# The borders between stages of a two-block network kernel on one core, and its expert scatter

## The chip, the cores and the metric

The kernel runs on one core of a Trainium2 chip. A core has TensorE (PE in the rows; PEld is its load of weights), VectorE (DVE), ScalarE (ACT), GpSimd (POOL) and SyncE (SP, which here only issues DMAs). The metric is the device time in microseconds (us) of one execution, as the median of several.

## The reference, cut to what matters

256 tokens of 1024 features, all fp32, pass through two blocks. The parts follow each other, and each border between two of them is a residual sum and a norm:

```python
def rmsnorm(x, g):
    xf = x.astype(jnp.float32)
    xf = xf * lax.rsqrt(jnp.mean(xf * xf, axis=-1, keepdims=True) + EPS)
    return (xf * g.astype(jnp.float32)).astype(x.dtype)

# block 1 (16 meta tokens in front; they are dropped at its end)
h = h + hybrid_mixer(rmsnorm(h, g_mix), ...)        # ends in  y @ w_out      (2048 -> 1024)
h = h + peer_ffn(rmsnorm(h, g_ffn), ...)            # ends in  act @ expert_v (16384 -> 1024)
h = rmsnorm(h, g_final)
# block 2
h = h + hgrn2_mixer(rms_norm(h, hg_norm), ...)      # ends in  o @ w_out
h = h + conv_ffn(rms_norm(h, ffn_norm[0]), ...)     # ends in  (silu(conv) * val) @ w_down
h = h + swa_sink_attention(rms_norm(h, attn_norm), shared_kv(h, kv_norm), ...)   # ends in  out @ w_o
h = h + conv_ffn(rms_norm(h, ffn_norm[1]), ...)
return rms_norm(h, final_norm)

# peer_ffn, its middle: 8 heads pick 16 of 16384 experts each, expert = i1 * 128 + i2
act = gelu(einsum('td,tkd->tk', xb, u)) * gates
out = einsum('tk,tkd->td', act, expert_v[experts])
```

So there are six such borders after the first norm: w_out to PEER, PEER to HGRN2 (two norms in a row: g_final, then hg_norm), HGRN2 to FFN 0, FFN 0 to attention, attention to FFN 1, and FFN 1 to the output.

## The kernel before, in words

**Slabs.** All weights come as a stream of 524 slabs of 128 x 1024 fp32. SP loads them into a ring of four. Each is split in two: ACT writes the rounded upper part (`split_hi`, L234) and DVE the remainder (`split_lo`, L242), three slabs ahead of their use. A product of two such splits takes three matmuls. An `up` slab (L258 to L260) makes 128 output features for all 256 tokens: 8 steps over k, 24 matmuls into one of two banks, which ACT or DVE must empty before its turn comes again. A `down` slab (L319 to L321) takes 128 input features and adds to all 1024 outputs of both token tiles: 12 matmuls into the four banks 4 to 7, which hold the sum over the whole stage. Its input y is split as well (yhi by ACT, ylo by DVE: L467 and L472; L1907 and L1944 in the FFNs), two slabs ahead.

**A border.** When the first token tile of the last down slab is done, DVE adds banks 4 and 5 to h, and after the slab banks 6 and 7 (`add_dve`, L451); it then splits one more slab. ACT squares and sums each tile of h (L372); DVE makes mean plus eps, ACT the root, DVE the reciprocal (L381, L376, L384), each for both tiles in one instruction; DVE scales tile 0 and ACT tile 1 (L391, L396). Then PE transposes 8 x 2 squares of 128 x 128 (`norm_pe`, L411) into banks 4 to 7, ACT multiplies by the gain into xhi (L430), DVE makes xlo (L437), and the first up slab may start, step k when part k of xlo is there. From PEER to HGRN2 the kernel does the sums, the mean and the root twice, with a product in between that writes the new h (L1701). There the old h is also fetched back from HBM: three DMAs on POOL's queue, the last of which waits for the last ylo.

**Clearing.** `clear_accumulators` (L302) runs four matmuls of one row of zeros over banks 4 to 7 ahead of each down stage, and PE waits until they are done. In the FFNs, where up and down slabs alternate, it stands between the first two up slabs.

**PEER.** 128 up slabs give the activations of all 16384 experts, which are stored to HBM; 128 down slabs use them. Beside up slabs 64 to 127 the gates are scattered: G, for token t and columns i1, i2, is a product of two one-hot matrices made from lists of 128 picks. In each of 64 steps there are one up slab and four tokens. DVE makes the left one-hot with the gate on it (L1378, one instruction a token, two buffers); POOL copies four columns (L1456) and makes the right one-hot (L1462, one instruction a token, four buffers); PE multiplies them (L1177), two tokens in the middle of the up slab and two behind it. ACT copies the result of four tokens, 128 x 512, to G (L1241), which is laid out token by token, so that later the factor of down slab k is read with a stride of 128 elements (L1398).

The order of work on each engine is the order of the code; semaphores tie the engines together. Loops are unrolled by four.

## Time and profile before

| | us |
|---|---|
| median of 3 runs | 1847.3 (1847.25 to 1850.32) |
| the profiled execution | 1850.21 |
| its span, first to last instruction | 1848.3 |
| PE busy in it | 1739.4 (94%) |
| DVE busy | 1266.9 (69%) |
| ACT busy | 962.1 (52%) |
| POOL busy | 415.7 (22%) |

In the rows, times are us from the span's start. PE's instructions overlap, so that the distance between two starts counts, not the length. "Idle before" is the idle time of that engine ahead of the instruction, with what ended it. PEclk is the granted TensorE clock as a share of 2.4 GHz.

### The profile page before, as it was taken

To read this page: it belongs to the slowest core of one execution; us is meant where nothing else is said; L and a number is where in the kernel's file an instruction comes from. 1 tells how busy PE (TensorE), PEld (TensorE's weight loads), DVE (VectorE), ACT (ScalarE), POOL (GpSimd) and SP (SyncE) were. 2 spreads that over 40 slices of the span, in tenths; PEclk is the share of its full clock that TensorE was granted. 3 is DMA by queue.
4 is the path that set the end of the run, shared out by engine and by line. 5 is a ranking of instruction groups with operands and counts; after the bars stand their busy time and mean duration, and the time that the engine had idled before them with its cause. 6 is when DMAs were issued, how large, how long until landed. Compare 5 with 4: busy or idle time off the path is not lost.

```text
span 1848.3 us, 36609 instructions
## 1 busy us (share of the span) xinstructions
PE 1739.4 (94%) x11651; PEld 1590.8 (86%) x11651; DVE 1266.9 (69%) x2118; ACT 962.1 (52%) x1455; POOL 415.7 (22%) x430
## 2 busy tenths in 40 slices
PE   7999999998989999999999998999899998789998
PEld 6998879998989999988888886988699998679997
DVE  5866664588976666678888887698566665556565
ACT  6653345666644444445555554654455555555554
POOL 0022300234268888810000000066000000100000
PEclk9999999999999999999999999999899999999999
DMA  5542255577764444567777777433255554135553
GB/s 182 169 137 81 74 188 182 166 211 212 214 193 163 156 157 158 166 209 240 242 242 241 241 241 247 142 119 110 100 161 183 184 189 132 35 119 187 185 181 112
DMA packets 114423, 316.59 MB, mean 171 GB/s; under 512 B 12768, under 2 KB 45920, under 8 KB 113984
## 3 DMA queue, kind: packets, MB, share of 16 engines
q1 hardware_dynamic: 113360, 311.88, 53.0%
q0 software_dynamic: 1008, 4.00, 0.7%
q8 instruction: 32, 0.52, 0.1%
q14 instruction: 23, 0.19, 0.0%
HBM read 296.95 MB, written 18.87 MB: 171 GB/s over the span
## 4 chain that ended last, share of the span: by engine, by line
PE 81%; DVE 10%; ACT 3%; issue 3%; POOL 2%; DMA 1%; POOLq 0%; DVEq 0%; ACTq 0%; SPq 0%
PE bank L258 13%; PE bank L260 13%; PE bank L259 13%; PE bank L319 10%; PE bank L320 10%; PE bank L321 10%; PE bank L1177 3%; DVE wlo L242 2%; POOL ylo L1462 1%; PE bank L1591 1%; PE bank L411 1%; DVE arena L1754 1%; PE bank L883 1%; ACT arena L372 1%; ACT whi L234 1%
## 5 line engine op out<-in xcount | busy, mean ns | idle before, releaser
L242 DVE TENSOR_TENSOR wlo<-raw,whi 128x1024 fp32r<-128x1024 f32 x502 | 640.1, 1277 | 199.2 <-ACT whi L234 189.5
L258 PE MATMUL bank<-xhi,whi 128*128 128x256 f32 (+1 forms) x2424 | 707.2, 292 | 15.9 <-DVE wlo L242 9.2
L260 PE MATMUL bank<-xhi,wlo 128*128 128x256 f32 (+1 forms) x2424 | 691.4, 285 | 0.0
L259 PE MATMUL bank<-xlo,whi 128*128 128x256 f32 (+1 forms) x2424 | 691.0, 285 | 0.0
L234 ACT ACTIVATE whi<-raw 128x1024 fp32r<-128x1024 f32 x524 | 550.9, 1052 | 116.1 <-PE bank L321 65.6
L258 PEld LDWEIGHTS bank<-xhi,whi 128*128 128x128 f32 x2424 | 468.1, 193 | 26.3 <-issue 13.7
L259 PEld LDWEIGHTS bank<-xlo,whi 128*128 128x128 f32 x2424 | 468.2, 193 | 1.7
L260 PEld LDWEIGHTS bank<-xhi,wlo 128*128 128x128 f32 x2424 | 467.3, 193 | 0.0
L319 PE MATMUL bank<-whi,yhi 128*128 128x512 f32 x816 | 322.2, 395 | 2.3 <-DVE ylo L1406 1.3
L320 PE MATMUL bank<-wlo,yhi 128*128 128x512 f32 x816 | 320.9, 393 | 0.0
L321 PE MATMUL bank<-whi,ylo 128*128 128x512 f32 x816 | 320.2, 392 | 0.0
L1462 POOL TENSOR_SCALAR ylo<-iota,tiny 128x128 fp32r<-128x128 f32 x256 | 214.1, 852 | 20.2 <-PE bank L1177 14.4
L319 PEld LDWEIGHTS bank<-whi,yhi 128*128 128x128 f32 x816 | 155.2, 190 | 36.6 <-DVE ylo L472 2.6
L321 PEld LDWEIGHTS bank<-whi,ylo 128*128 128x128 f32 x816 | 155.0, 190 | 32.8
L320 PEld LDWEIGHTS bank<-wlo,yhi 128*128 128x128 f32 x816 | 155.2, 190 | 30.3
L1214 ACT ACTIVATE h<-bank 128x256 f32<-128x256 f32 x128 | 49.1, 384 | 206.2 <-PE bank L260 206.0
L1259 ACT ACTIVATE yhi<-h 128x256 fp32r<-128x256 f32 x128 | 53.4, 418 | 173.2 <-PE bank L321 169.5
L1378 DVE TENSOR_SCALAR h<-iota,h 128x128 f32<-128x128 f32 x256 | 85.8, 368 | 73.6 <-PE bank L1177 73.0
L1406 DVE TENSOR_TENSOR ylo<-h,yhi 128x256 fp32r<-128x256 f32 x128 | 54.4, 425 | 68.0 <-ACT yhi L1259 68.0
L1177 PE MATMUL bank<-ylo,h 128*128 128x128 f32 x512 | 84.3, 282 | 11.4 <-POOL ylo L1462 11.4
L1927 DVE SCALAR_TENSOR_TENSOR arena<-bank,vec,arena 128x255 f32<-128x255 f32 x88 | 42.4, 482 | 71.8 <-ACT arena L1892 65.8
L1437 POOL TENSOR_TENSOR wlo<-raw,whi 128x1024 fp32r<-128x1024 f32 x22 | 53.5, 2432 | 145.3 <-ACT whi L234 121.6
(255 smaller groups left out, 1563.5 us busy)
## 6 DMA issues: line engine op xcount, KB each, us to landing
raw<-in_stream SPq DMA_DIRECT2D x524, 512.0 KB, 3.5
act_spill<-h SPq DMA_DIRECT2D x128, 128.0 KB, 3.2
h<-act_spill SPq DMA_DIRECT2D x128, 128.0 KB, 3.4
h<-in_x SPq DMA_DIRECT2D x1, 1024.0 KB, 5.1
arena<-in_keys POOLq DMA_DIRECT2D x1, 1024.0 KB, 5.9
h_spill<-h SPq DMA_DIRECT2D x1, 1024.0 KB, 8.5
out<-arena SPq DMA_DIRECT2D x2, 512.0 KB, 2.7
h<-h_spill POOLq DMA_DIRECT2D x2, 256.0 KB, 5.1
```

The costliest lines, as they stand in the source:

```text
L234: nc.scalar.activation(whi[:, q * 1024:(q + 1) * 1024], raw[:, q * 1024:(q + 1) * 1024], ACT.Copy).then_inc(hi_ready, 1)
L242: nc.vector.tensor_tensor(wlo[:, q * 1024:(q + 1) * 1024], raw[:, q * 1024:(q + 1) * 1024], whi[:, q * 1024:(q + 1) * 1024].bitcast(F32), ...
L258: nc.tensor.matmul(bank[b][:, 0:T], whi[:, w], xhi[:, x], start=k == 0, stop=False)
L259: nc.tensor.matmul(bank[b][:, 0:T], whi[:, w], xlo[:, x], start=False, stop=False)
L260: last = nc.tensor.matmul(bank[b][:, 0:T], wlo[:, w], xhi[:, x], start=False, stop=k == KT - 1)
L319: nc.tensor.matmul(o, yhi[:, y], whi[:, w], start=False, stop=False, skip_group_check=True)
L320: nc.tensor.matmul(o, yhi[:, y], wlo[:, w], start=False, stop=False, skip_group_check=True)
L321: last = nc.tensor.matmul(o, ylo[:, y], whi[:, w], start=False, stop=True, skip_group_check=True)
L1177: nc.tensor.matmul(o, HOT1[:, y % 2 * P:(y % 2 + 1) * P], HOT2[:, y * P:(y + 1) * P].bitcast(F32), start=True, stop=True).then_inc(s("hot_ ...
L1378: nc.vector.tensor_scalar(HOT1[:, y % 2 * P:(y % 2 + 1) * P], iota[:, :], c1(I1T), c1(GT_COLS), ALU.is_equal, ALU.mult).then_inc(s("hot_a" ...
L1406: nc.vector.tensor_tensor(ylo[:, yq * SEQ:(yq + 1) * SEQ], PRD[:, yq * SEQ:(yq + 1) * SEQ], yhi[:, yq * SEQ:(yq + 1) * SEQ].bitcast(F32), ...
L1462: nc.gpsimd.tensor_scalar(HOT2[:, y * P:(y + 1) * P], iota[:, :], PCOL[:, y:y + 1], None, ALU.is_equal).then_inc(s("hot_b"), 1)
```

## The change: borders tile by tile, and the scatter's right one-hot on VectorE

It does six things.

1. The last two down slabs of a stage are taken together: both for token tile 0, then both for tile 1 (`down_last`). A semaphore tells of each of banks 4, 5 and 6, and the last slab's own of bank 7.
2. The norm of a border goes by tile, and for tile 1 by half (`turn_dve`, `turn_act`, `turn_pe`): tile 0 has its own root, reciprocal, scaling and transposes. Eps goes into ACT's bias. The transposes go to banks 2 to 6. The split of slab last + 3 stands after the norm on both engines, not in the middle of it and ahead of it.
3. From PEER to HGRN2 the two norms are one: DVE multiplies the sum by g_final (u), ACT squares and sums both h and u, and the root is of a combination of the two sums. The new residual is made later, beside the second and third HGRN2 slabs. The old h and g_final are fetched when 52 of the 128 products of the down stage are made, into a part of G that is used up by then.
4. The output is multiplied by its gain before the root is known, and leaves in three DMAs.
5. No clearing matmuls: the first down matmul into each bank starts it anew.
6. The right one-hots of four tokens are made by one DVE instruction, a comparison of iota and the columns, both broadcast, into two buffers of four tokens (ylo and yhi) in turn. POOL does none of it. ACT writes G transposed, expert by expert, and the factor of down slab k is contiguous.

```diff
+        def down_last(pe, n, d):
+            for tt in range(TT):
+                for z in range(2):
+                    q, yq = slot(n + z, 0), (d + z) % 2
+                    if tt == 0:
+                        pe.wait_ge(lo_ready, n + z + 1)
+                        pe.wait_ge(y_lo, d + z + 1)
+                    y = slice(yq * SEQ + tt * P, yq * SEQ + (tt + 1) * P)
+                    for nh in range(2):
+                        last = down_half(bank[4 + 2 * tt + nh][:, :], y, nh, q, False)
+                        if z and 2 * tt + nh < 3:
+                            last.then_inc(bank_done, 1)
+                    if tt:
+                        last.then_inc(slabs_done, 1)
...
+            add(0)
+            add(1)
+            gain(0, D, 1)
+            add(2)
+            gain(D, D + 512, 2)
+            if a == T_HG:
+                dve.wait_ge(turn_ss, ss_base(a) + 2)
+                nc.vector.scalar_tensor_tensor(out=TV[:, 0:1], in0=TSS[:, 0:1], scalar=EPS, in1=TSS[:, 1:2],
+                                               op0=ALU.mult, op1=ALU.add).then_inc(turn_v, 1)
+            add(3)
+            gain(D + 512, 2 * D, 3)
+            dve.wait_ge(turn_rt, 2 * a + 1)
+            nc.vector.reciprocal(TRS[:, 0:1], TRT[:, 0:1]).then_inc(turn_rs, 1)
+            dve.wait_ge(turn_rs, 2 * a + 1)
+            nc.vector.tensor_scalar(nt[:, 0:D], turn_src(a)[:, 0:D], TRS[:, 0:1], None, ALU.mult)\
+                .then_inc(turn_nt, 1)
+            dve.wait_ge(turn_ss, ss_base(a + 1))
...
+            act.wait_ge(h_done, 4 * a + 2)
+            square(0, D, 0)
+            square_u(0, D, 0, 1)
...
+            act.wait_ge(h_done, 4 * a + 3)
+            square(D, D + 512, 2)
+            square_u(D, D + 512, 2, 2)
+            act.wait_ge(h_done, 4 * a + 4)
+            square(D + 512, 2 * D, 4)
+            square_u(D + 512, 2 * D, 4, 3)
...
+            pe.wait_ge(h_done, 4 * a + 4)
+            pe.wait_ge(turn_nt, 2 * a + 1)
+            for j in range(KT):
+                nc.tensor.transpose(turned(j)[:, 0:P], nt[:, j * P:(j + 1) * P], ident[:, :])
+            pe.wait_ge(turn_nt, 2 * a + 2)
+            for j in range(KT):
+                if j == KT // 2:
+                    pe.wait_ge(turn_nb, a + 1)
+                last = nc.tensor.transpose(turned(j)[:, P:SEQ], nt[:, D + j * P:D + (j + 1) * P], ident[:, :])
...
-                dst = G[:, k * w:(k + 1) * w] if isinstance(k, int) else G[:, bass.ds(k * w, w)]
-                nc.scalar.activation(dst, bank[2 + r % 2][:, 0:w], ACT.Copy).then_inc(s("g_evac"), 1)
+                n = (i * 4 + r) * TPS
+                g3 = G[:, :].rearrange("p (k t) -> p t k", t=SEQ)
+                dst = g3[:, n:n + TPS, :] if isinstance(n, int) else g3[:, bass.ds(n, TPS), :]
+                nc.scalar.activation(dst, bank[2 + r % 2][:, 0:TPS * KEYS].rearrange("p (t k) -> p t k", k=KEYS),
+                                     ACT.Copy).then_inc(s("g_evac"), 1)
...
+            def four_tokens(k0, i, r):
+                n = i * (4 * TPS) + (k0 + r) * TPS
+                c4 = I2T[:, n:n + TPS] if isinstance(n, int) else I2T[:, bass.ds(n, TPS)]
+                nc.vector.tensor_tensor(HOT2[(k0 + r) % 2][:, :].rearrange("p (t k) -> p t k", k=P),
+                                        iota[:, :].unsqueeze(1).to_broadcast([P, TPS, P]),
+                                        c4.unsqueeze(2).to_broadcast([P, TPS, P]),
+                                        ALU.is_equal).then_inc(s("hot_b"), 1)
...
-            for part, free, count in ((slice(6 * SEQ, 8 * SEQ), s("hot_free"), SEQ + TPS), (slice(0, 4 * SEQ), y_new, KEYS),
-                                      (slice(4 * SEQ, 6 * SEQ), y_lo, D_V + KEYS)):
-                pool.wait_ge(free, count)
-                pool.dma_start(h[:, part], t["h_spill"][:, part]).then_inc(s("h_back"), 16)
+            pool.wait_ge(y_new, 13 * D // SEQ)
+            pool.dma_start(H_OLD, t["h_spill"]).then_inc(s("h_back"), 16)
+            pool.dma_start(G_FINAL, t["g_final"]).then_inc(s("row_in"), 16)
```

PE at the first border, w_out to PEER, in program order. Before (L321 is the last matmul of the last down slab, L411 the transposes, L258 the first up matmul):

```order
L321 MATMUL bank<-whi,ylo 128x512
L112 REGISTER_ALU
L112 COMPARE_AND_BRANCH
L411 MATMUL bank<-ident,arena 128x128 [waits nt_done]
L411 MATMUL bank<-ident,arena 128x128 x15
L258 MATMUL bank<-xhi,whi 128x256 [waits nlo_done,up_evac,lo_ready]
```

And now (L303 the last down matmul, L542 the transposes of tile 0, L547 those of tile 1, L259 the first up matmul):

```order
L303 MATMUL bank<-whi,ylo 128x512
L542 MATMUL bank<-ident,arena 128x128 [waits turn_nt,h_done]
L542 MATMUL bank<-ident,arena 128x128 x7
L547 MATMUL bank<-ident,arena 128x128 [waits turn_nt]
L547 MATMUL bank<-ident,arena 128x128 x3
L547 MATMUL bank<-ident,arena 128x128 [waits turn_nb]
L547 MATMUL bank<-ident,arena 128x128 x3
L259 MATMUL bank<-xhi,whi 128x256 [waits nlo_done,up_evac,lo_ready]
```

One wait for both tiles became three, and the transposes of tile 0 stand ahead of the wait for tile 1.

DVE at the same border. Before (L451 the sums, L242 a slab's split, L381 and L384 the mean and the reciprocal, L391 the scaling of tile 0, L437 xlo):

```order
L242 TENSOR_TENSOR wlo<-raw,whi 128x1024 [waits hi_ready]
L451 TENSOR_TENSOR h<-h,bank 128x512 [waits halves_done]
L451 TENSOR_TENSOR h<-h,bank 128x512
L451 TENSOR_TENSOR h<-h,bank 128x512 [waits slabs_done]
L451 TENSOR_TENSOR h<-h,bank 128x512
L242 TENSOR_TENSOR wlo<-raw,whi 128x1024 [waits hi_ready]
L381 TENSOR_SCALAR tiny<-tiny 128x2 [waits ss_done]
L384 RECIPROCAL tiny<-tiny 128x2 [waits rt_done]
L391 TENSOR_SCALAR arena<-h,tiny 128x1024 [waits rs_done]
L437 SCALAR_TENSOR_TENSOR xlo<-bank,vec,xhi 128x256 [waits nhi_done] x8
```

And now (L452 the sums, L472 to L474 root, reciprocal and scaling of tile 0, L483 to L487 those of tile 1, L570 xlo, L243 the split):

```order
L243 TENSOR_TENSOR wlo<-raw,whi 128x1024 [waits hi_ready]
L452 TENSOR_TENSOR h<-h,bank 128x512 [waits bank_done] x3
L452 TENSOR_TENSOR h<-h,bank 128x512 [waits slabs_done]
L472 RECIPROCAL tiny<-tiny 128x1 [waits turn_rt]
L474 TENSOR_SCALAR arena<-h,tiny 128x1024 [waits turn_rs]
L483 TENSOR_TENSOR tiny<-tiny 128x1 [waits turn_ss]
L485 RECIPROCAL tiny<-tiny 128x1 [waits turn_rt]
L487 TENSOR_SCALAR arena<-h,tiny 128x512 [waits turn_rs]
L570 SCALAR_TENSOR_TENSOR xlo<-bank,vec,xhi 128x256 [waits nhi_done] x8
L243 TENSOR_TENSOR wlo<-raw,whi 128x1024 [waits hi_ready]
```

The split of slab last + 3 moved from behind the sums to behind xlo.

DVE in a step of the scatter, now (L1488 the left one-hot of a token, L1494 the right ones of the next step's four; before, the rows were the same without L1494):

```order
L1488 ISA [waits hot_free]
L1488 TENSOR_SCALAR h<-iota,h 128x128
L242 ISA
L243 TENSOR_TENSOR wlo<-raw,whi 128x1024 [waits hi_ready]
L1486 REGISTER_ALU
L1488 ISA [waits hot_free]
L1488 TENSOR_SCALAR h<-iota,h 128x128
L1486 REGISTER_ALU
L1488 ISA [waits hot_free]
L1488 TENSOR_SCALAR h<-iota,h 128x128
L1494 ISA
L1494 TENSOR_TENSOR yhi<-iota,h 128x512
```

The added comparison stands behind the second pair of tokens and ahead of the next step's first.

## Rows read from the trace of the kernel before

**Rows 1.** The page, the chain that ended last, by engine:

```profile
PE 81%; DVE 10%; ACT 3%; issue 3%; POOL 2%; DMA 1%; POOLq 0%; DVEq 0%; ACTq 0%; SPq 0%
```

**Rows 2.** Waits of the whole program: who for whom, total us, times, longest:

```profile
PE bank L411 <- ACT arena L396: 29.2, 5, 11.7
PE bank L1177 <- POOL ylo L1462: 11.4, 15, 2.0
```

**Rows 3.** PE in one turn of the scatter's loop: start, length, instruction, idle before:

```profile
614.87 0.38 PE L258 MATMUL bank<-xhi,whi 128*128 128x256 f32 x1
...
617.75 0.36 PE L258 MATMUL bank<-xhi,whi 128*128 128x256 f32 x1
...
619.64 0.36 PE L258 MATMUL bank<-xhi,whi 128*128 128x256 f32 x1
...
631.42 0.38 PE L258 MATMUL bank<-xhi,whi 128*128 128x256 f32 x1
```

**Rows 4.** Groups of instructions from 540 to 780 us (busy, mean ns, idle before):

```profile
L1378 DVE TENSOR_SCALAR h<-iota,h 128x128 f32<-128x128 f32 x236 | 79.2, 368 | 66.6 <-PE bank L1177 66.4
L242 DVE TENSOR_TENSOR wlo<-raw,whi 128x1024 fp32r<-128x1024 f32 x59 | 74.3, 1260 | 24.2 <-ACT whi L234 24.2
L234 ACT ACTIVATE whi<-raw 128x1024 fp32r<-128x1024 f32 x59 | 62.2, 1054 | 1.6
L1241 ACT ACTIVATE arena<-bank 128x512 f32 x59 | 34.6, 587 | 0.0
L1214 ACT ACTIVATE h<-bank 128x256 f32<-128x256 f32 x59 | 22.6, 383 | 130.4 <-PE bank L260 130.4
```

**Rows 5.** Single lines of the program: ns min/median/max, first and last start:

```profile
L1298 DVE TENSOR_TENSOR arena<-arena x16: 417/422/1870, 384.9 to 493.5; 128x256 f32<-128x256 f32 x16
L1318 DVE TENSOR_TENSOR arena<-iota,arena x4: 2284/2285/2286, 414.3 to 507.6; 128x2048 f32<-128x2048 f32 x4
L1398 DVE TENSOR_TENSOR h<-h,arena x128: 595/629/642, 796.4 to 1140.7; 128x256 f32<-128x256 f32 x128
```

**Rows 6.** The border from HGRN2 to FFN 0, in order of time:

```profile
1333.22 0.39 PE L321 MATMUL bank<-whi,ylo 128*128 128x512 f32 x1
...
1336.78 1.15 ACT L396 ACTIVATE arena<-h,tiny 128x1024 f32<-128x1024 f32 x1 [0.23 <-DVE tiny L384]
1336.78 0.75 DVE L391 TENSOR_SCALAR arena<-h,tiny 128x1024 f32<-128x1024 f32 x1
1337.98 3.68 PE L411 MATMUL bank<-ident,arena 128*128 128x128 f32 x16 [4.38 <-ACT arena L396]
...
1340.01 3.44 DVE L437 SCALAR_TENSOR_TENSOR xlo<-bank,vec,xhi 128x256 fp32r<-128x256 f32 x8 [2.47 <-ACT xhi L430]
...
1341.31 0.56 PE L258 MATMUL bank<-xhi,whi 128*128 128x256 f32 x1
...
1345.55 1.04 PE L302 MATMUL bank<-tiny 1*128 1x512 bf16 x4
...
1346.65 0.39 PE L258 MATMUL bank<-xhi,whi 128*128 128x256 f32 x1
```

**Rows 7.** The border from PEER to HGRN2:

```profile
1147.63 0.39 PE L321 MATMUL bank<-whi,ylo 128*128 128x512 f32 x1
...
1163.00 0.42 PE L258 MATMUL bank<-xhi,whi 128*128 128x256 f32 x1
...
1167.96 0.38 ACT L1636 ACTIVATE arena<-bank 128x256 f32<-128x256 f32 x1
```

**Rows 8.** The end of FFN 0, and the end of the program:

```profile
1528.45 0.47 PE L319 MATMUL bank<-whi,yhi 128*128 128x512 f32 x1 [0.15 <-DVE ylo L1944]
...
1842.70 2.48 DVE L2154 SCALAR_TENSOR_TENSOR arena<-h,tiny,arena 128x1024 f32<-128x1024 f32 x2
```

**Rows 9.** Stretches: PE, PEld, DVE, ACT, POOL busy (count), PEclk, DMA share, GB/s:

```profile
1340.00:1344.00 4.00, 4.00 (x20) 4.00 (x19) 3.92 (x9) 3.45 (x7) 0.00 (x0) 0.50 0.07 27
940.00:960.00 20.00, 20.00 (x90) 16.57 (x89) 16.21 (x23) 9.65 (x15) 0.00 (x0) 1.00 0.75 243
```

461 lines of the change are left out of this document (241 added, 220 removed).

## The prediction

> **What bounds the kernel now.** I read the page first: the chain that ended last is PE for 81%, DVE for 10% [rows 1]. So PE's work is the bound, and what can be won is where PE stands idle or works at half clock. The waits say where [rows 2]: PE's transposes (L411) waited 29.2 us for the norm's last scaling at five borders, 11.7 of them at one, so 4.4 us at each of the four others; and the scatter's matmuls (L1177) waited 15 times for POOL. Then I read these places in order of time [rows 3, 6, 7], and for each resource that the change uses more the groups, single lines and stretches [rows 4, 5, 9]. In the down stage of PEER, and in the long up loops, PE does not wait (20.00 us busy of 20.00 in rows 9), so faster DVE work there is worth nothing.
>
> **The scatter.** A half step (12 up matmuls and two tokens) takes PE 619.64 - 617.75 = 1.89 us without a wait, and 617.75 - 614.87 = 2.88 with the wait for POOL [rows 3]. There is one such wait in each turn of four steps, which takes 631.42 - 614.87 = 16.55 us. 14 waits of this kind (the 15th is the first step's, 2.0 us, rows 2) at 1.0 are 14.0 us. What is late next, once POOL is out? DVE gets one comparison of 512 elements a step. The nearest row is L1318, the same comparison of two broadcasts on 2048 elements, 2285 ns, so 571 ns for 512 [rows 5]. A step's DVE work becomes 4 x 0.37 + 1.26 + 0.57 = 3.3 us [rows 4] against PE's 3.78. The comparison stands where DVE now waits for PE before the next token (66.4 us over 236 tokens, 1.1 us a step, rows 4), needs no buffer that PE has not long left, and so costs nothing up to about 1 us. ACT writes G with a stride of 1 KB: the price is in no row. Its bounds: 0.59 us as now [rows 4], and above, as the strided read L1398 is to the contiguous L1298 (629 to 422 ns, rows 5), 0.88 us; three times as much, 1.8 us, would still fit, since ACT has 1.05 + 0.59 us and a copy of 0.4 in a step of 3.78. I take 0.6 to 0.9, no cost. The first step's wait of 2.0 us shrinks to what DVE needs for its comparison, about 0.4: 1.6 won. Sum 15.6 us. Ends: 8 (DVE or ACT sometimes late by half a us) and 18 (halves just behind the stall, a tenth late, become normal as well).
>
> The Trainium skill speaks against the strided write: in "SBUF — State Buffer", section "Door 1: The DMA port swizzle", each access that crosses to a new 16-byte line pays a penalty, and an fp32 stride of over four elements does so every time. The read with a stride of 128 elements shows such a penalty on DVE, a half more [rows 5]; no row shows a write by ACT. By the rule the read gets cheaper and the write dearer; both stay beside PE's work, so the sum would be the same by the one as by the other.
>
> **One plain border, worked out on HGRN2 to FFN 0** [rows 6]. T is the end of the last down matmul, 1333.61. Before: scaling at T+3.2, the transposes at T+4.4 and the first up matmul at T+7.7; an up slab at full clock takes 2.85 us (24 x 0.119, half a step less its tokens), so it ends at T+10.5. After, with a sum of 512 columns 0.65 us, a square of 1024 columns 1.2 and of 512 0.75, a root, a reciprocal and each handover 0.2: banks 4 and 5 are done at T-3.4 and T-2.7; DVE is still at a split and has both sums at T-1.4; ACT's square and root end at T+0.2; DVE has bank 6's sum at T and bank 7's at T+0.7; reciprocal, then 0.75 for scaling tile 0 [rows 6]: T+1.65. PE starts its transposes at T+1.7 instead of T+4.4. ACT meanwhile squares the two halves of tile 1 until T+1.5; sum, root, reciprocal, and the half scalings on DVE and ACT together end at T+2.9, while PE is at tile 0 (8 x 0.2). PE ends the transposes at T+4.9. xlo then sets the pace, 3.44/8 = 0.43 a part against PE's 0.36: its first part is there at T+4.6, its last at T+7.9, and the first up slab ends at T+8.2. Won: 2.3 us. Ends: 1.2, if half clock falls on the up slab, and 3.
>
> The clock: in this border it was at 0.50 over 4 us after PE had been idle for 4.38 [rows 6, 9], and the first up slab took 1345.46 - 1341.31 = 4.15 us. After the shorter idle time of 1.7 us it may fall or not; I count on full clock in the up slab here (1.3 more won) and let the range hold the other case.
>
> What the moved split gives back: on ACT behind xhi now stand two splits, so that in the FFNs the convolution's first product comes at T+9.1, not at once, and DVE, with two splits behind xlo, ends its two taps at T+11.6. They empty the bank for the third up slab, which PE could start at T+11.0: 0.6 lost at both FFN borders. In PEER and attention ACT's copy comes at T+9.5, in time.
>
> The six borders: w_out to PEER 2.3. HGRN2 to FFN 0: 2.3 + 1.3 - 0.6 = 3.0. Attention to FFN 1: 2.3 - 0.6 = 1.7. FFN 0 to attention: here the last down slab began at 1528.45, when its ylo came, about 3.1 us after the slab before it had begun [rows 8], for DVE makes a split before this ylo. Now that ylo is wanted 1.36 us (half a down slab) after that beginning, so PE waits there, and 18 matmuls, not 12, stand behind it: 6 x 0.227 = 1.4 lost, 0.9 left. FFN 1 to output has no split there: 0.25 lost.
>
> PEER to HGRN2 [rows 7]: T is 1148.02. Before: first up matmul at T+15.0, and the third slab, which needs the Sigmoid of the first (ends at 1168.34, T+20.3), right behind the second, at T+20.8. After: h is there early, so no DMA ends any wait. The products with g_final (0.65 for 512 columns, 1.2 for 1024) and the squares of u double both engines' lists: tile 0 is scaled at T+3.2, tile 1 at T+5.8, the first up matmul at T+7.4. But ACT then has a split, two roots, the load of two function tables and another split ahead of the Sigmoid, DVE a split ahead of the small lower-bound work that ACT's Exp waits for: xhi ends at T+9.5, Sigmoid at T+15.4. So the third slab begins at T+15.5: 5.3 won, not the 7.6 that the first up matmul shows. Ends: 4 and 7.
>
> Output: before, the last scaling ended at 1842.70 + 2.48 = T+5.7 [rows 8] and the span 3.1 later. After, the chain goes add, gain, square, sum, root, reciprocal, half scaling: T+4.35, but SP issues three DMAs one behind the other (about 0.7 each), the last at T+5.0: 0.7 won, less the 0.25 above: 0.5.
>
> **No clearing.** From the clearing's start to the next up matmul 1346.65 - 1345.55 = 1.1 us [rows 6]; it is on PE's path in both FFNs and ahead of w_out: 3.3. Ahead of the HGRN2 and attention down stages PE waits for ylo beside it, 0.4 each. Ahead of PEER's down stage ylo comes 1.3 later anyway: 0. Sum 4.1.
>
> **Fetching h and g_final early** puts 1.5 MB into a stage that uses 0.75 of the DMA engines' time [rows 9]. The spare quarter of 243/0.75 = 324 GB/s takes it in about 19 us, and the loads run four slabs ahead. Cost 0; if it is not spread so, at most 1.5 MB / 243 GB/s = 6.5 us.
>
> **Sum.** 15.6 + 2.3 + 5.3 + 3.0 + 0.9 + 1.7 + 0.5 + 4.1 = 33.4 us. The profiled execution took 1850.2 (span 1848.3 and 1.9 around it), so 1816.8; the median shown is 2.9 below that execution, so the forecast is 1813.9 us.
>
> **The rivals.**
> - The scatter wins little: four tokens in turn hand work from PE to DVE and back, and with POOL gone the next stall is DVE's (its split waits 24.2 us for ACT, rows 4, and the tokens behind it are close to late). For it: that closeness. Against: three of four turns already run at 1.89 with all of this. With 8 of the 15.6 lost, 1821.9.
> - Half clock moves from the transposes, which are short, into the up slabs: five borders at 1.2 more, and HGRN2's, about 7 us: 1821. For it: rows 9 show the clock down for the length of a slab after one idle time. Against: the idle time falls from 4.38 to 1.7.
> - The early fetch delays the weights: 6.5 us, 1820.4. Against it: the spare quarter.
> - Slower than before: ACT's write of G is so dear that it sets the step. It decides from 3.78 - 1.05 - 0.38 = 2.35 us for 512 elements [rows 4]; the other gains (17.8 us, 0.28 a step) are eaten when a step takes 4.14 + 0.28 = 4.42, so at 3.0 us, 5.8 ns an element against 1.15 now. At 3.5 us a step is 4.93, and 64 x 0.79 - 17.8 = 33 more than now: 1880. For it: nothing but that no row shows the case. Against: the strided read is only 1.5 times dearer.
>
> In "TensorE: Matmul & The Clock Gate", section "HAM oscillation", the Trainium skill has the clock fall only where idle gaps are long, and by that the new borders would all run at full clock: some 2 us more won, 1812. Rows 9 agree that the clock fell behind the long gap; no row has one of 1.7 us at a border.
>
> **How the numbers follow.** The sum as it stands, within 5 us: 0.62. The scatter short: 0.14. The clock: 0.10. The fetch: 0.05. More than one of them: 0.04. The slow write: 0.05, of which 0.02 ends within 0.2% (3.7 us, about what a measurement tells from no change) and 0.03 above. So faster by over 0.2% 0.95, the same 0.02, slower 0.03. The range is 1805 (scatter 18, borders at their better ends) to 1825 (two of the three smaller mishaps).
>
> **What the profile after would show.** In the scatter: POOL absent, turns of 15.4 to 15.6 us, no wait of L1177 but the first, the comparison at 0.55 to 0.65 us, L1241's successor at 0.6 to 0.9. At each border: transposes from T+1.7, a first up slab ending near T+8.2, PEclk at 1.00 in it. At FFN 0's end a wait of 1.6 us in the middle of the paired slabs; at HGRN2 a third slab at T+15.5; at the FFNs a third up slab 0.6 late. The prediction is wrong if a step stays at 4.1 us, if the write of G takes over 2.3, or if PE waits in PEER's down stage near 940 us.

## The result, and where the time went

| | median of device us | lowest to highest |
|---|---|---|
| before | 1848.6 | 1847.3 to 1850.3 (4 runs) |
| changed | 1804.8 | 1802.6 to 1805.9 (4 runs) |
| ratio | 0.9761 | 95% interval 0.9744 to 0.9778 |

The changed kernel is 43.8 us faster. Forecast were 33.4 us and 1813.9; the measured time is just below the low end of the range (1805.0). The profiled executions span 1848.3 and 1800.2 us, so 48.1 lie between the two traces: the profiled execution of before took 1850.2 us, 1.6 above its median, that of the changed kernel 1802.6, 2.2 below its own. The page of the changed kernel names the same bound with a larger share [rows 1]:

```profile
PE 83%; DVE 11%; ACT 3%; issue 2%; DMA 0%; POOL 0%; ACTq 0%; DVEq 0%; SPq 0%; POOLq 0%
```

To see where the 48.1 us lie, take every eighth of the matmuls of L258 (now L259), the start of an up slab, and the first of each down slab, and subtract its start in the one trace from its start in the other. Both kernels have the same 303 up slabs and 204 down slabs in the same order, so the difference only moves where one kernel is quicker:

| place | difference before and behind it, us | won | forecast |
|---|---|---|---|
| start to w_out | 0 to 1.5 | 1.5 | 0 |
| w_out, first three down slabs | 1.5 to 3.2 | 1.7 | 1.1 (clearing) |
| border w_out to PEER | 3.2 to 6.0 | 2.8 | 2.3 |
| one up slab at 432 us | 6.0 to 7.5 | 1.5 | 0 |
| scatter, with the start of PEER's down stage | 7.5 to 29.4 | 21.9 | 15.6 |
| border PEER to HGRN2 | 29.4 to 35.7 | 6.4 | 5.3 |
| HGRN2's down stage | 35.7 to 35.6 | -0.1 | 0.4 |
| border HGRN2 to FFN 0, with one clearing | 35.6 to 40.9 | 5.3 | 4.1 |
| border FFN 0 to attention | 40.9 to 42.4 | 1.5 | 0.9 |
| attention's down stage | 42.4 to 44.2 | 1.8 | 0.4 |
| border attention to FFN 1, with one clearing | 44.2 to 47.9 | 3.7 | 2.8 |
| end | 47.9 to 48.1 | 0.2 | 0.5 |

Two things stand out at once. The scatter gave 6.3 more than its term. And 1.5 to 1.8 us each came in four places where the change does nothing or next to nothing (the start, w_out, one up slab at 432 us, attention's down stage); with them the gain looks larger than it is.

**Scatter.** PE in one turn of the loop, start, length, instruction [rows 3]:

```profile
600.30 0.36 PE L259 MATMUL bank<-xhi,whi 128*128 128x256 f32 x1
...
604.06 0.36 PE L259 MATMUL bank<-xhi,whi 128*128 128x256 f32 x1
...
615.34 0.36 PE L259 MATMUL bank<-xhi,whi 128*128 128x256 f32 x1
```

A step takes 3.76, a turn 15.04 us, every one; not 15.4 to 15.6. The groups from 540 to 780 us in the same columns as [rows 4], then the two lines new to the trace (ns min/median/max). The scatter now ends at 766 us, so the last 14 us of this stretch belong to the next stage:

```profile
L243 DVE TENSOR_TENSOR wlo<-raw,whi 128x1024 fp32r<-128x1024 f32 x63 | 77.2, 1225 | 29.9 <-ACT whi L235 29.9
L1488 DVE TENSOR_SCALAR h<-iota,h 128x128 f32<-128x128 f32 x240 | 72.2, 344 | 19.4 <-PE bank L1288 17.8
```

```profile
L1494 DVE TENSOR_TENSOR ylo<-iota,h x32: 681/685/691, 525.4 to 757.4; 128x512 fp32r<-128x512 f32 x32
L1351 ACT ACTIVATE arena<-bank x64: 1023/1092/1126, 529.9 to 766.0; 128x512 f32 x60, 128x512 f32<-128x512 f32 x4
```

The comparison takes 0.69 us (0.57 estimated: a quarter of the 2048-element row leaves out the part that does not shrink, for 2285 and 685 ns are 1.04 ns an element and 0.15 us besides), the strided write of G 1.09 (bounds 0.59 to 0.88, so above them, but far from 2.35). DVE's waits for PE fell from 66.4 to 17.8 us: the new comparison (40.5 us in this stretch) filled most of them, as said.

**A plain border**, HGRN2 to FFN 0 [rows 6]. T is 1298.04; scaling starts at T+0.8, transposes at T+1.7:

```profile
1297.65 0.39 PE L303 MATMUL bank<-whi,ylo 128*128 128x512 f32 x1
...
1298.87 0.75 DVE L474 TENSOR_SCALAR arena<-h,tiny 128x1024 f32<-128x1024 f32 x1
...
1299.77 1.07 PE L542 MATMUL bank<-ident,arena 128*128 128x128 f32 x8 [1.73 <-DVE arena L474]
1300.82 1.09 PE L547 MATMUL bank<-ident,arena 128*128 128x128 f32 x8
1302.32 0.36 PE L259 MATMUL bank<-xhi,whi 128*128 128x256 f32 x1 [0.41 <-DVE xlo L570]
...
1305.74 0.28 PE L259 MATMUL bank<-xhi,whi 128*128 128x256 f32 x1
```

The idle time is 1.73 instead of 4.38 us, and 1.73 to 1.74 at the other three plain borders too. The first up slab ends at T+7.7. So it does at two of the other three; at attention to FFN 1 half clock covers part of it, and it ends at T+8.3, 0.55 us later (columns of [rows 9]):

```profile
1603.00:1607.00 4.00, 4.00 (x25) 3.74 (x24) 3.78 (x9) 4.00 (x9) 0.00 (x0) 0.66 0.02 4
```

ACT and DVE at HGRN2 to FFN 0:

```profile
1301.18 3.03 ACT L561 ACTIVATE xhi<-bank,vec 128x256 fp32r<-128x256 f32 x8 [0.19 <-PE bank L547]
...
1305.94 0.62 ACT L2000 ACTIVATE arena<-bank,vec 128x256 f32<-128x256 f32 x1
```

```profile
1307.47 0.99 DVE L2034 SCALAR_TENSOR_TENSOR arena<-bank,vec,arena 128x255 f32<-128x255 f32 x2
```

**PEER to HGRN2** [rows 7], T = 1118.67: first up matmul at T+7.0, third slab at T+14.4, right behind the first of the Sigmoids (the load of their table stands ahead of it):

```profile
1118.28 0.39 PE L303 MATMUL bank<-whi,ylo 128*128 128x512 f32 x1
1122.05 1.94 PE L542 MATMUL bank<-ident,arena 128*128 128x128 f32 x8 [3.38 <-DVE arena L474]
...
1125.64 0.55 PE L259 MATMUL bank<-xhi,whi 128*128 128x256 f32 x1
...
1133.07 0.39 PE L259 MATMUL bank<-xhi,whi 128*128 128x256 f32 x1 [0.45 <-ACT arena L1738]
```

**FFN 0's end** [rows 8]: the foretold wait between the paired slabs, and the starts of the down stages, where clearing used to stand:

```profile
215.49 0.47 PE L301 MATMUL bank<-whi,yhi 128*128 128x512 f32 x1 [1.01 <-DVE ylo L585]
768.61 0.47 PE L301 MATMUL bank<-whi,yhi 128*128 128x512 f32 x1 [2.63 <-DVE ylo L1529]
1274.06 0.76 PE L301 MATMUL bank<-whi,yhi 128*128 128x512 f32 x1 [1.82 <-DVE ylo L585]
1487.50 0.47 PE L301 MATMUL bank<-whi,yhi 128*128 128x512 f32 x1 [1.51 <-DVE ylo L2051]
1577.01 0.47 PE L301 MATMUL bank<-whi,yhi 128*128 128x512 f32 x1 [1.59 <-DVE ylo L585]
```

**Stretches** [rows 9]: in the first up slab of FFN 0 the clock is 1.00 (before, 0.50), and PE does not wait in PEER's down stage while the early fetch runs (issued at 905 us; DMA share 0.89, 316 GB/s):

```profile
1302.00:1306.00 4.00, 3.62 (x27) 3.45 (x28) 3.78 (x9) 4.00 (x10) 0.00 (x0) 1.00 0.02 4
905.00:925.00 20.00, 20.00 (x90) 16.57 (x89) 14.19 (x23) 9.84 (x15) 1.12 (x2) 1.00 0.89 316
```

### The profile page after: what moved, and what is told of

Read it like the earlier page. It is cut to its first block, busy times and chain, and to the rows that moved or that the text cites. A ratio compares the mean times of both kernels' runs of the same rounds, so it can differ in the third digit from the quotient of the medians.

```text
span 1800.2 us, 35518 instructions
## 1 busy us (share of the span) xinstructions
PE 1717.4 (95%) x11627; PEld 1576.6 (88%) x11627; DVE 1275.4 (71%) x2201; ACT 995.2 (55%) x1476; POOL 188.5 (10%) x108
## 4 chain that ended last, share of the span: by engine, by line
PE 83%; DVE 11%; ACT 3%; issue 2%; DMA 0%; POOL 0%; ACTq 0%; DVEq 0%; SPq 0%; POOLq 0%
PE bank L259 14%; PE bank L260 14%; PE bank L261 14%; PE bank L301 10%; PE bank L302 10%; PE bank L303 10%; PE bank L1288 3%; DVE wlo L243 2%; DVE arena L1860 1%; PE bank L1691 1%; PE bank L996 1%; ACT whi L235 1%; DVE arena L1876 1%; DVE arena L1408 1%; DVE h L452 1%
## 5 line engine op out<-in xcount | busy, mean ns | idle before, releaser
L243 DVE TENSOR_TENSOR wlo<-raw,whi 128x1024 fp32r<-128x1024 f32 x502 | 637.5, 1273 | 218.6 <-ACT whi L235 206.5
L259 PE MATMUL bank<-xhi,whi 128*128 128x256 f32 (+1 forms) x2424 | 707.0, 292 | 14.6 <-DVE wlo L243 7.8
L259 PEld LDWEIGHTS bank<-xhi,whi 128*128 128x128 f32 x2424 | 466.8, 193 | 23.5 <-issue 13.4
L303 PE MATMUL bank<-whi,ylo 128*128 128x512 f32 x816 | 319.3, 391 | 0.0
L303 PEld LDWEIGHTS bank<-whi,ylo 128*128 128x128 f32 x816 | 154.3, 189 | 32.7
L1488 DVE TENSOR_SCALAR h<-iota,h 128x128 f32<-128x128 f32 x256 | 77.0, 344 | 20.3 <-PE bank L1288 18.7
L2034 DVE SCALAR_TENSOR_TENSOR arena<-bank,vec,arena 128x255 f32<-128x255 f32 x88 | 42.4, 482 | 68.8 <-ACT arena L2000 62.5
L2000 ACT ACTIVATE arena<-bank,vec 128x256 f32<-128x256 f32 x44 | 24.9, 567 | 85.3 <-PE bank L261 85.3
L1351 ACT ACTIVATE arena<-bank 128x512 f32 (+1 forms) x64 | 70.1, 1095 | 0.1
```

Of the source, the lines that this page charges most:

```text
L243: nc.vector.tensor_tensor(wlo[:, q * 1024:(q + 1) * 1024], raw[:, q * 1024:(q + 1) * 1024], whi[:, q * 1024:(q + 1) * 1024].bitcast(F32), ...
L259: nc.tensor.matmul(bank[b][:, 0:T], whi[:, w], xhi[:, x], start=k == 0, stop=False)
L303: return nc.tensor.matmul(o, ylo[:, y], whi[:, w], start=False, stop=True, skip_group_check=True)
L1351: nc.scalar.activation(dst, bank[2 + r % 2][:, 0:TPS * KEYS].rearrange("p (t k) -> p t k", k=KEYS), ACT.Copy).then_inc(s("g_evac"), 1)
L1488: nc.vector.tensor_scalar(HOT1[:, y % 2 * P:(y % 2 + 1) * P], iota[:, :], c1(I1T), c1(GT_COLS), ALU.is_equal, ALU.mult).then_inc(s("hot_a" ...
```

## The experiments

All medians stand beside runs of the kernel before on the same chip. A border is worth 1 to 6 us and the intervals are some 3 us to either side, so where less than that is at stake the verdict comes from the trace, at the place in question.

### Why the scatter gave 22 us: POOL was full

The waits charged to POOL add up to 11.4 us [rows 2], and my term made of them was 15.6, yet the stage became 22.3 shorter from the start of the 126th up slab of the program to that of the last in PEER (532.13 to 791.74 before, 524.67 to 761.98 now). What I had not read in the trace of before is POOL's own row in the same 240 us (from 540 to 780; busy, mean ns, idle before):

```profile
L1462 POOL TENSOR_SCALAR ylo<-iota,tiny 128x128 fp32r<-128x128 f32 x234 | 196.1, 854 | 18.6 <-PE bank L1177 14.1 <-POOL tiny L1456 4.5
L1456 POOL COPY tiny<-h 128x4 f32 x59 | 11.0, 186 | 14.6 <-POOL ylo L1462 14.6
```

196.1 + 18.6 + 11.0 + 14.6 = 240.3: it never rests, but for gaps of 0.2 to 0.4 us between its own instructions. The 14.1 us that the row charges to PE, and the 4.5 beside them, are one such gap per step, behind the copy. POOL in order of time:

```profile
602.42 0.19 POOL L1456 COPY tiny<-h 128x4 f32 x1 [0.24 <-POOL ylo L1462]
602.90 3.43 POOL L1462 TENSOR_SCALAR ylo<-iota,tiny 128x128 fp32r<-128x128 f32 x4 [0.30 <-POOL tiny L1456]
606.58 0.19 POOL L1456 COPY tiny<-h 128x4 f32 x1 [0.25 <-POOL ylo L1462]
```

So this step of POOL takes 0.19 + 0.30 + 3.43 + 0.24 = 4.16 us (on average its copies stand 4.10 us apart), and PE's 3.76. Three experiments tell this from the other readings.

**The new scatter alone, in the kernel before.**

```diff
-        HOT2 = ylo
+        HOT2 = (ylo, yhi)
...
+                four_tokens(1, i, r)          # DVE, as in the change; G written by key
...
-            steps(pool, KEYS - E1, 4, step)   # POOL's comparisons
```

> The kernel before with the new scatter alone (comparison of four tokens on DVE into two buffers, G written by key); borders, clearing and late fetch as before. Theory A, POOL's pace: before, POOL's own list for a step (four comparisons 3.4 us, the copy 0.19, and its handovers of about 0.24 and 0.30) takes 4.14 us, PE's work 3.76, so every one of some 62 steps was 0.36 to 0.38 too long, whatever wait the profile names. Then a turn of four steps takes 15.04 us and this kernel is 21 to 23 us faster than before (about 1826). Theory B, my forecast: only the named waits go, a turn takes 15.4 to 15.6 and the gain is 15.6 us (1833).

Measured 1825.5 us beside 1849.3 (ratio 0.9875, 0.9845 to 0.9906): 23.9 us. The same two slabs are 237.30 us apart, 22.3 less than before, and every turn takes 15.04. Theory A.

**POOL with two buffers.**

```diff
-        HOT2 = ylo
+        HOT2 = (ylo, yhi)
...
-            pe.sem_inc(s("hot_free"), TPS)
+            pe.sem_inc(s("hot_free"), 2 * TPS)
...
-    nc.gpsimd.tensor_scalar(HOT2[:, y * P:(y + 1) * P], iota[:, :], PCOL[:, y:y + 1], None,
+    nc.gpsimd.tensor_scalar(HOT2[r % 2][:, y * P:(y + 1) * P], iota[:, :], PCOL[:, y:y + 1], None,
```

> The kernel before, POOL still compares token by token, but into two buffers in turn, so that it may run a whole step ahead of PE. Theory A, POOL's pace: nothing is gained, POOL needs 4.1 us a step with any number of buffers; turn 16.3 to 16.6 us, time within 2 us of before. Theory C, the single buffer: the stall came from POOL waiting for PE to free the buffer; then a turn takes 15.0 to 15.2 and the gain is about 20 us.

Measured 1846.1 (ratio 0.9991, 0.9975 to 1.0007): no change. The two slabs are 259.34 us apart (before 259.61), turns 16.36 to 16.56. A second buffer gives POOL room to run ahead, and it never does.

```profile
602.99 0.19 POOL L1456 COPY tiny<-h 128x4 f32 x1 [0.25 <-POOL yhi L1462]
603.48 3.39 POOL L1462 TENSOR_SCALAR ylo<-iota,tiny 128x128 fp32r<-128x128 f32 x4 [0.30 <-PE bank L1177]
607.12 0.19 POOL L1456 COPY tiny<-h 128x4 f32 x1 [0.25 <-POOL ylo L1462]
```

The row still says "<-PE bank" before the comparisons, though PE had freed that buffer a whole step earlier: the 0.30 us are as long where the row says "<-POOL tiny", so they are POOL's own, whatever the label.

**POOL on half the columns, one buffer.**

```diff
-    nc.gpsimd.tensor_scalar(HOT2[:, y * P:(y + 1) * P], iota[:, :], PCOL[:, y:y + 1], None,
+    nc.gpsimd.tensor_scalar(HOT2[:, y * P:y * P + P // 2], iota[:, 0:P // 2], PCOL[:, y:y + 1], None,
```

> The kernel before, one buffer, but POOL compares only 64 of the 128 columns of each token (the other half of the one-hot is left out). Theory A, POOL's pace: its four comparisons take 1.8 to 2.6 us instead of 3.4, its step 2.5 to 3.3 us is under PE's 3.76, a turn takes 15.04 and the gain is 21 to 23 us, though the buffer is single. Theory C, the single buffer: each comparison still has to wait for PE's token of the step before, and at least half of the stall stays: turn 15.8 to 16.4, gain under 10 us.

Measured 1827.0 (ratio 0.9881, 0.9853 to 0.9910): 22.3 us, turns of 15.04, slabs 239.07 apart. That is 20.5 of the 22.3 us between the slabs; the rest is the first step, which takes 5.95 us here, 6.26 before and 4.19 with the new scatter. A comparison takes 0.50 instead of 0.85 us on average, and now POOL really waits for PE:

```profile
L1462 POOL TENSOR_SCALAR ylo<-iota,tiny 128x64 fp32r<-128x64 f32 x244 | 115.0, 499 | 43.2 <-PE bank L1177 28.2 <-POOL tiny L1456 15.1
```

With POOL's step shorter than PE's the whole gain per turn is there, single buffer and all. That POOL's pace was the bound is shown, from both sides.

**What POOL's step is made of.** The average of 0.85 us hides two kinds of comparison. In the trace of before, from 540 to 780 us (ns min/median/max):

```profile
L1462 POOL TENSOR_SCALAR ylo<-iota,tiny x234: 594/603/1740, 540.0 to 779.6; 128x128 fp32r<-128x128 f32 x117
```

Most take 0.60 us. The rest, 58 of them, about one a step, take 1.3 to 1.7, and each of these runs beside a split of DVE and ends 0.4 to 0.5 us behind it. The last two comparisons of the step above, 0.60 and 1.62 us, and the split:

```profile
604.13 2.20 POOL L1462 TENSOR_SCALAR ylo<-iota,tiny 128x128 fp32r<-128x128 f32 x2
```

```profile
604.64 1.23 DVE L242 TENSOR_TENSOR wlo<-raw,whi 128x1024 fp32r<-128x1024 f32 x1 [0.65 <-ACT whi L234]
```

With half the columns the same hold falls on POOL's copy, which takes 1.10 us (median) instead of 0.19. So about 1.0 of POOL's 4.16 us is time in which DVE's split keeps it out; four comparisons of 0.60, the copy and the gaps are 3.1 us by this estimate, less than PE's 3.76. POOL was the bound only together with that hold. Whether the old scatter would have kept PE's pace with the split out of its way is a rival to moving the comparison, and no run tests it.

### The gains where nothing was changed: the clock's own time

**The changed kernel again.**

> The changed kernel once more, for its second trace and its time beside the others. If the granted clock falls where the instruction stream puts it, the half clock stretches stand at the same times as in the first trace (150.7, 224.4, 420.8, 769.7, 1274.6, 1510.7 us) and the spans agree within 0.5 us. If the clock keeps a time of its own, they stand elsewhere, and unchanged code (the slabs at 132, 226 and 432 us before) differs by 1.5 us each between two executions of the same kernel. Time 1802 to 1807 us either way.

Measured 1805.5 beside 1849.3 (ratio 0.9755, 0.9728 to 0.9783), again 43.8. The span is 1804.7, 4.5 us more than the first trace of the very same kernel, and those 4.5 us are in place before PEER: by 0.6 at 24 us, 1.6 at 213, 3.9 at 234, 4.5 at 281. From there to the end the two traces stay within 0.6 of that. (The 0.6 come while the early fetch runs, which cost nothing in the first trace: at 920 us a product of DVE waits for its row of the spill, and PE 0.3 us for ylo.)

```profile
920.09 0.42 DVE L1522 TENSOR_TENSOR h<-h,arena 128x256 f32<-128x256 f32 x1 [2.76 <-DMA h<-act_spill]
```

The half clock stretches are what moved. From 131 to 137 us three kernels execute the same instructions within 2 us of each other; the columns are those of [rows 9], the first line is before, the second the changed kernel's first trace, the third the late fetch (below):

```profile
131.00:137.00 6.00, 6.00 (x30) 4.86 (x30) 0.00 (x0) 2.62 (x5) 2.76 (x1) 0.72 0.23 79
```

```profile
131.00:137.00 6.00, 6.00 (x35) 4.51 (x34) 0.71 (x2) 3.78 (x7) 2.77 (x1) 1.00 0.21 79
```

```profile
131.00:137.00 6.00, 6.00 (x30) 5.12 (x29) 0.00 (x0) 2.72 (x5) 2.76 (x1) 0.72 0.09 37
```

The late fetch is identical to the changed kernel up to 905 us, and has the clock of the kernel before. Likewise the slab at 432 us of before, with nothing new near it, ran at a clock of 0.58 over 4 us, and the kernel with the scatter alone at 1.00 in the same place. So did the kernel before with two POOL buffers, which differs from it in the scatter only (before, then two buffers):

```profile
432.00:436.00 4.00, 3.72 (x19) 3.73 (x20) 3.83 (x17) 0.67 (x1) 1.06 (x1) 0.58 0.58 164
```

```profile
432.00:436.00 4.00, 4.00 (x35) 4.00 (x34) 3.79 (x18) 2.64 (x4) 2.40 (x1) 1.00 0.82 257
```

That trace tells whose luck it was. It has the old code in all four places, and yet it is quicker than the trace of before by 1.3, 1.5, 1.6 and 1.6 us in them (in the order of the sum below: the slab at 132 us, the slab at 432 us, w_out, attention's down stage). Three of the four pieces, all but the one in w_out, are in the second trace of the changed kernel as well. So it is the one trace of before that was unlucky there. In "TensorE: Matmul & The Clock Gate", section "What's actually happening", the Trainium skill says that the window over which activity is judged runs freely and does not start with the kernel; that the stretches move between executions agrees, though no run here shows why. So 1.5 (all up to w_out) + 1.5 + 1.6 (of the 1.7 in w_out) + 1.6 (of the 1.8 in attention's down stage) = 6.2 of the 48.1 us between the two traces are luck, and 41.9 are the change's by this account. The medians, 43.8 apart in both comparisons, lie between; their interval (41 to 47) holds the 41.9.

### The borders, one edit at a time

**Clearing put back.**

```diff
+            clear_accumulators(pe, ...)
-            down(pe, n0, d0, 0, 0, 4, first=True)
+            down(pe, n0, d0, 0, 0, 4)
```

> The changed kernel with the four clearing matmuls put back at all six places (before a down stage, and after the first up slab of each FFN). My forecast priced them at 4.1 us: 1.1 ahead of w_out and in both FFNs, 0.4 ahead of the HGRN2 and attention down stages. The trace of the changed kernel says less: ahead of w_out, PEER, HGRN2 and attention PE now waits 1.01, 2.63, 1.82 and 1.59 us for ylo, longer than clearing takes, so only the two in the FFNs should cost, 2 x 1.1 = 2.2 us, and the first down matmuls of the other stages should come when they come now.

Measured 1809.0 (ratio 0.9786, 0.9761 to 0.9811). In the trace the second up slab of the FFNs comes 1.2 us later in both; ahead of w_out the first down matmul comes 4.84 us behind the start of the last up slab (4.88 in the second trace of the changed kernel), ahead of HGRN2's down stage it comes within 0.15 of when it came, and ahead of PEER the wait for ylo is 1.66 instead of 2.63, with clearing in the rest. Ahead of attention's down stage it comes 1.6 us later than in the second trace of the changed kernel, counted from the second up slab; the kernel with yhi and ylo first (below), which has no clearing, loses 1.5 there, so this is again half clock. So no clearing is worth 2.4 us by the traces, not 4.1: at four of six places it stood in PE's wait for ylo. (The medians are 3.5 to 4.2 apart, with intervals too wide to tell that from 2.4.)

**Slab by slab.**

```diff
-            for tt in range(TT):
-                for z in range(2):
+            for z in range(2):
+                for tt in range(TT):
```

> The changed kernel with the last two down slabs taken one after the other, as before; the norm by tile and half stays. Theory P, the pairing brings the early transposes: tile 0's banks are then complete 1.36 us later, and transposes at every border start 1.36 later; with the wait of 1.5 at FFN 0's end gone the sum is 5 x 1.36 - 0.1 = about 6.5 us slower than the changed kernel (1811). Theory D, the chain is set by DVE's four sums, which end at T+0.7 in either order: square of tile 0 from T-0.7, root by T+0.9, scaling by T+1.9, so transposes at T+2.0 to 2.1 instead of T+1.7; 0.3 to 0.4 lost at four borders, about 0.9 at PEER to HGRN2, 1.4 won at FFN 0's end: within 1.5 us of the changed kernel.

Measured 1806.0 (ratio 0.9778, 0.9756 to 0.9800), within 1 us of the changed kernel. The same wait as above, from its trace, at PEER to HGRN2 and HGRN2 to FFN 0:

```profile
1126.06 1.94 PE L539 MATMUL bank<-ident,arena 128*128 128x128 f32 x8 [4.37 <-DVE arena L471]
1302.01 1.06 PE L539 MATMUL bank<-ident,arena 128*128 128x128 f32 x8 [2.01 <-DVE arena L471]
```

2.01 instead of 1.73, and 0.3 more between the tiles' transposes: 0.5 to 0.9 us at each plain border and 1.0 at PEER to HGRN2, 3.6 in all, against 1.5 won at FFN 0's end and 0.4 at FFN 1's. (0.6 more are lost in PEER's down stage, in the place of the early fetch named above, which the pairing does not touch.) The waits are those of theory D, the sum of 1.7 us is just above its 1.5: the early transposes come from the norm by tile and half, and the pairing adds little.

**The split ahead of the norm again** (on top of slab by slab).

```diff
+            split_hi(act, D_END[a] - 1 + AHEAD, 0, 0, 4)     # turn_act, ahead of the squares
+            split_lo(dve, D_END[a] - 1 + AHEAD, 0, 0, 4)     # turn_dve, behind the sums
...
-            split_hi(act, n0 - 1 + AHEAD, 0, 0, 4)           # behind xhi
-            split_lo(dve, n0 - 1 + AHEAD, 0, 0, 4)           # behind xlo
```

> The kernel with the last two slabs one after the other, and the split of the third next slab ahead of the norm again, as before: on ACT before the first square (where ACT idles anyway), on DVE between the four sums and the first reciprocal (1.23 us). Theory S, moving the split behind xlo is a real part of the gain: DVE's reciprocal, scaling and PE's transposes come 1.2 us later at all five borders (wait of about 3.2 us instead of 2.0), 5 to 6 us in all: about 1812. Theory G, my forecast's debit: the split given back behind xlo had made the third up slab 0.6 late in the FFNs, so part of it returns, and the sum is about 4.5. No third slab is late in the trace of the changed kernel (steps of 2.88 to 2.94 us behind the first), so S.

Measured 1813.5 (ratio 0.9809, 0.9793 to 0.9826), 7.4 us above slab by slab, of which the trace gives 3.4 to the borders: PE's wait ahead of the transposes is 2.87 us at all four plain ones instead of 2.01, and the slabs behind come 0.88, 0.33 (PEER to HGRN2), 0.78, 0.82 and 0.57 us later. The other 3.8 of the 7.2 us between the spans lie in unchanged code (half clock, as above, and 0.4 at the early fetch). Theory S has the mechanism, but 0.86 a border instead of 1.2.

```profile
275.60 1.14 PE L541 MATMUL bank<-ident,arena 128*128 128x128 f32 x8 [2.87 <-DVE arena L472]
```

**Late fetch.**

```diff
-            pool.wait_ge(y_new, 13 * D // SEQ)
+            pool.wait_ge(y_new, KEYS)
```

> The changed kernel, but h and g_final are fetched only when the product for the last key is made. Theory F, the early fetch is what shortens PEER to HGRN2: the product stands some 4 us before the end T of the last down matmul, the 1 MB takes 5.9 us and g_final behind it more, so the first sum starts about T+3 instead of T-2.9 and everything behind it, third slab included, comes about 6 us later; time about 1811. Theory N, folding the two norms is what counts and the fetch is hidden anyway: less than 2 us later. In PEER's down stage no wait appears or goes in either.

Measured 1809.3 (ratio 0.9796, 0.9770 to 0.9822). PE's wait ahead of the transposes is 8.06 us instead of 3.38, and DVE's sums stand behind the DMA:

```profile
1125.72 1.28 DVE L452 TENSOR_TENSOR h<-arena,bank 128x512 f32<-128x512 f32 x2 [4.59 <-DMA arena<-in_g_final]
```

Theory F has the mechanism, at 4.7 us instead of about 6: 4.7 of the 6.4 us of this border hang on the early fetch. Without it the folded norm is worth only the rest, 1.7.

**G laid out as before** (on top of the late fetch; by token, all of G is in use until the last key, so there is no room for an early one).

```diff
-                dst = g3[:, n:n + TPS, :]
+                dst = G[:, k * w:(k + 1) * w]
...
-                gk = G[:, k * SEQ:(k + 1) * SEQ]
+                gk = gk[:, :, k:k + 1]
```

> The kernel of the late fetch, with G laid out as before: ACT writes 512 contiguous elements (0.59 us instead of 1.09), DVE reads 256 with a stride (0.63 us instead of 0.42). By both theories the scatter's turn stays at 15.04 us, for ACT and DVE have room, and the down stage's slabs stay at 2.72 us. Theory 1, the layout costs nothing but the last write: the first down matmul of PEER comes 0.5 us sooner after the last scatter matmul, and the rest agrees with the late fetch within 0.5 us. Theory 2, the strided writes hold PE up somewhere: this kernel is 2 us or more faster than the late fetch.

Measured 1807.7 (ratio 0.9781, 0.9759 to 0.9803). The wait at the start of the down stage is 2.38 instead of 2.63 us, and the border's first up matmul 0.4 earlier; the slabs between are the same. ACT's write takes 584 ns, DVE's product 630. Theory 1: the layout costs 0.3 us by itself, 0.6 if the 0.4 at the border are its own, which no run shows. It buys the room for the early fetch, which my working never connected with it.

### Three tries at a better kernel

**yhi and ylo ahead of the split**, in the last step of an FFN.

```diff
-                if not first:
+                if not first and not final:
                     split_lo(dve, n + 2 + AHEAD, i, 0, 12)
...
+                if final:
+                    split_lo(dve, n + 2 + AHEAD, i, 0, 12)
```

> The changed kernel, but in the last step of each FFN ACT and DVE make yhi and ylo before the split that stands ahead of them. DVE's ylo then ends at about the 12th matmul before, 1.1 to 1.4 us earlier, and PE's wait of 1.51 us in the paired slabs of FFN 0 falls to 0.2 or nothing; FFN 1 has no split there and stays. Expected: 1.3 to 1.5 us less than the changed kernel (1804), seen in the trace at that place rather than in the medians. Rival: the delayed split makes the next stage's weights late, and the wait comes back in the first up slabs of attention.

Measured 1805.1 (ratio 0.9764, 0.9748 to 0.9780). The wait of 1.51 us at FFN 0's end is gone (1.4 won there, none of it given back at attention's start). The 1805.1 beside 1804.8 and 1805.5 do not show it.

The other waits left are in PEER, at 414 to 426 and 502 to 515 us: a split of DVE takes 3.3 to 4.1 us while a product of POOL runs (DVE, then POOL, in the changed kernel):

```profile
416.58 4.07 DVE L243 TENSOR_TENSOR wlo<-raw,whi 128x1024 fp32r<-128x1024 f32 x1
...
422.14 4.03 DVE L243 TENSOR_TENSOR wlo<-raw,whi 128x1024 fp32r<-128x1024 f32 x1
...
427.65 1.23 DVE L243 TENSOR_TENSOR wlo<-raw,whi 128x1024 fp32r<-128x1024 f32 x1
```

```profile
414.03 11.05 POOL L1567 TENSOR_TENSOR arena<-arena 128x2048 f32<-128x2048 f32 x2 [11.51 <-DVE arena L1428]
```

POOL's two products end at about 419.5 and 425.1, the splits 1.1 us behind each. **Products on DVE** (on top of the last one):

```diff
-            return k % 2 == 1 and (k < 24 or 30 <= k < 50)
+            return k % 2 == 1 and k < 62
...
-                    nc.gpsimd.tensor_tensor(e4, e4, lists...)
+                nc.vector.tensor_tensor(e4, e4, lists...)        # in one_hots
```

> The kernel f1, and POOL's four products of 2048 elements (11 us for two, at 414 and 502 us) are made by DVE right behind the one-hots; POOL takes every second split instead. In the trace of the changed kernel DVE's split takes 4.07, 4.03, 3.3 and 3.3 us instead of 1.23 while one of POOL's products runs, and PE then waits 2.41, 0.89, 1.50 and 2.40 us for wlo. Theory K, the two engines share a way to memory and POOL's product holds DVE up: splits go back to 1.2 us, DVE's product takes about 2.3 us, PE's waits of 7.5 us go, time 7 us under f1 (about 1796). Theory L, DVE is simply overloaded there: with the products added, it is later still, and the waits grow to 10 us or more.

Measured 1802.6 (ratio 0.9749, 0.9733 to 0.9766). Every split of DVE takes 1.22 us again, but PE still waits 8.3 us for wlo from 400 to 530 us (9.3 in the kernel above): DVE now carries the products, and two of its own large instructions take 4.35 and 4.5 us instead of 2.3 beside POOL's splits. Both theories are half right. The hold goes both ways: POOL's split beside the 2.29 us comparison at 419 us takes 4.35 us instead of 2.4.

**Short products.**

```diff
-                    nc.gpsimd.tensor_tensor(e4, e4, lists...)
+                    for x in range(PH):
+                        ins = nc.gpsimd.tensor_tensor(e4[:, x:x + 1], e4[:, x:x + 1], lists[:, x:x + 1]..., ALU.mult)
```

> The kernel f1 (POOL keeps its four products, DVE's order in the last FFN step as in f1), but each product of 2048 elements is issued as eight of 256. Theory K, an instruction of POOL on this path keeps DVE's out until it ends, and DVE's tensor_tensor waits at the door: then DVE's splits at 416 to 426 and 505 to 515 us wait for one short piece (0.7 us) instead of the rest of 5.5 us, take 1.3 to 2.0 us instead of 3.3 to 4.1, PE's waits for wlo of 7.0 us in these places fall under 1.5, and the time is about 6 us under f1 (1799). Theory M, POOL's pieces follow each other so closely that DVE does not get in between: splits stay at 3.3 to 4.1 us and the time stays at 1804 or rises by what eight instructions cost more than one.

Measured 1806.9 (ratio 0.9775, 0.9760 to 0.9790). Splits take 1.48 to 1.59 us and the first two waits of PE are gone, as theory K has it; but POOL's sixteen short products now take 15.0 us where the two long ones took 11.05, its own split comes behind them, and PE waits for that (POOL, then PE):

```profile
414.92 15.02 POOL L1568 TENSOR_TENSOR arena<-arena 128x256 f32<-128x256 f32 x16 [11.51 <-DVE arena L1428]
429.91 2.33 POOL L1558 TENSOR_TENSOR wlo<-raw,whi 128x1024 fp32r<-128x1024 f32 x1
```

```profile
432.37 0.58 PE L259 MATMUL bank<-xhi,whi 128*128 128x256 f32 x1 [3.92 <-POOL wlo L1558]
```

The stall moved by three slabs, and PE's waits for wlo from 400 to 530 us add up to 8.3 us, as with the products on DVE. None of the three is told apart from the changed kernel by its time; the products on DVE have the lowest median, 1802.6 beside 1804.8 and 1805.5, with intervals that overlap.

## Why the prediction was right, and where it failed

- **The scatter: the step that failed.** "14 waits of this kind at 1.0 are 14.0 us" takes a turn of 16.55 us to have one stall of 1.0, and three steps that "already run at 1.89" a half. The turn itself says otherwise: 16.55 against 4 x 3.76 = 15.04 are 1.51 lost, of which the named stall is two thirds; the rest stood in starts a tenth or three tenths late, charged to ACT or to nothing. I had the right kind of thing in the bounds ("halves just behind the stall, a tenth late, become normal as well", 18) and undersized it as well. The reason is that I summed PE's waits for POOL and never set POOL's cycle (4.10 to 4.16) beside PE's (3.76). That difference over 62 steps gives 21 to 25 us at once. Measured were 22.3: 2.1 in the first step (1.6 said) and 20.2 in the other 62 (14.0 said). This one term, 6.3 us short, is most of the miss of 10.4 in the gain. The forecast time missed by 9.1, because before's median, 1847.3 when I wrote, is 1848.6 with a fourth run; so the time lies only 0.2 us below the range, which hides how far the term was off.
- **Why POOL was slow was missed as well.** About 1.0 of its 4.16 us is DVE's split keeping it out once a step. The mean of 0.85 us a comparison hides it; the minimum and the median (0.59, 0.60) beside the maximum (1.74) show it.
- **The rival on DVE** (its split becomes the next stall) did not come, nor did the slow write: 1.09 us is 1.9 times the contiguous write, where the strided read is 1.5 times, and both lie beside PE. That the layout also makes the early fetch possible was missed.
- **The plain border: right within 0.6 us.** Transposes at T+1.7 as forecast; they end at T+3.9, not T+4.9, since 8 take 1.07 us at full clock where I had 1.6; so the first up slab ends at T+7.7 instead of T+8.2, and 2.8 are won instead of 2.3. The up slab ran at full clock at HGRN2 to FFN 0, as counted on, but not everywhere: behind the same 1.73 us of idle time half clock fell on the first up slab at one plain border in the first trace of the changed kernel and at two in the second (0.70 to 0.71 over the slab), at 0.55 to 0.6 us each. So the rival of the clock is real, at half its price of 1.2 and not at every border, and the expectation of full clock at all of them did not hold.
- **The debit for the moved split: wrong.** The third up slab of the FFNs was to be 0.6 late. ACT's first product came at T+7.9, not T+9.1 (xhi 3.03 us instead of 3.40, and earlier), DVE's taps ended at T+10.4, not T+11.6, and PE never waited. Put back in the old place the split costs 3.4 us.
- **FFN 0's end: right.** 1.51 us of wait (1.6 said), 1.5 won at that border (0.9 said).
- **PEER to HGRN2: mechanism right, 1.1 short.** Transposes at T+3.4 (T+3.2 said), third slab at T+14.4 (T+15.5 said), since xhi ended at T+8.9 (T+9.5 said) and ACT took 5.5 us from there to the end of the Sigmoid, not 5.9. 4.7 of the gain hang on the early fetch.
- **No clearing: 2.4 instead of 4.1.** I priced the place before w_out from the FFN row and did not ask what PE would wait for there next; ylo answers it (1.01 us).
- **The early fetch** cost 0 to 1.1 us in PEER's down stage (0 said): its 50 down slabs around 920 us take 136.0 us in every trace without it, and 136.0 to 137.1 in the eight traces with it.
- **The clock's 6.2 us** (between the spans; less between the medians) are in no term and could not be. They are luck of the profiled executions, and a range made of terms alone is too narrow by such a piece.

## What to carry over

Where an engine of the loop is busy in every slice, set its own cycle (its instructions and its own gaps) beside that of the bound engine, and multiply the difference by the number of steps; the waits charged to it are only the part of the loss that the trace can label. Look at the spread of its instructions and not at their mean alone: if some take far longer than the shortest, see what runs beside them. Before an instruction on PE's path is priced, ask which wait stands behind it. And two traces of one program differ by several us in where half clock falls, so compare marks stage by stage, and take a piece in unchanged code for luck until second traces of both programs have it too. A second trace of the changed kernel alone would have misled here: it has three of the four lucky pieces.

## What the runs showed of the hardware

- The clock falls at different places in executions of the same program: 0.72 or 1.00 over the same instructions at 131 to 137 us, 4.5 us between the spans of two traces of the changed kernel.
- Behind an idle time of 1.73 us, at the eight plain borders of two traces of the changed kernel, PE ran its next up slab at full clock at five, and at a clock of 0.60 to 0.75 over 4 us at three.
- ACT's copy of 128x512 fp32 out of the bank takes 1.09 us with a stride of 1 KB in its output and 0.58 without.
- A TENSOR_TENSOR of POOL (5.5 us) keeps one of DVE out until it ends: 4.07 instead of 1.23 us; POOL's splits do the same to DVE's products (4.35 instead of 2.29). In "SBUF — State Buffer", section "Who interferes with whom", the Trainium skill calls this an exclusive lock on a shared port; the end of DVE's split 1.1 us behind the end of POOL's product agrees, which is about its own length without the wait. It holds the other way round too: a comparison of POOL of 0.60 us takes 1.3 to 1.7 when it meets DVE's split of 1.23 us, and ends 0.4 to 0.5 us behind it. With POOL silent in the scatter, DVE's splits there went from 1260 to 1225 ns and its one-hots from 368 to 344.
- A comparison of POOL takes 0.60 us for 128 columns and 0.48 for 64 (medians; the means of 0.85 and 0.50 contain those that DVE held up), and POOL leaves 0.24 to 0.37 us between two dependent instructions.
